# DeltaNet's head norms on one Trainium2 core: the sum of squares as two fp32r products over the high and low parts

## The reference

```python
def l2_normalize(x):
    xf = x.astype(jnp.float32)
    return xf * lax.rsqrt(jnp.sum(xf * xf, axis=-1, keepdims=True) + L2_EPS)

qkv = jax.nn.silu(causal_depthwise_conv(qkv, conv_w))
q, k, v = jnp.split(qkv, [GDN_QK_DIM, 2 * GDN_QK_DIM], axis=-1)
q = l2_normalize(q.reshape(B, T, 16, 128))
k = l2_normalize(k.reshape(B, T, 16, 128))
```

## Time and profile before

| | us |
|---|---|
| median of 3 runs | 2800.21 (2799.41 to 2800.48) |
| the profiled execution | 2803.94 |
| its span, first to last instruction | 2802.1 |
| PE busy | 2739.6 (98%) |
| DVE busy | 2219.6 (79%) |
| ACT busy | 1648.4 (59%) |
| mean granted TensorE clock | 0.995 |

### The profile page before, as it was taken

The page is one execution under the profiler, slowest core; times in us unless marked ns, Lnnn a source line. Parts: engine busy times, 40 slices in busy tenths (PEclk is TensorE's granted clock), DMA queues, the critical chain, the costliest instruction groups (busy, mean ns, idle before and its releaser), DMA issues.

```text
span 2802.1 us, 40252 instructions
## 1 busy us (share of the span) xinstructions
PE 2739.6 (98%) x13456; PEld 2282.1 (81%) x13456; DVE 2219.6 (79%) x2727; ACT 1648.4 (59%) x2184; POOL 31.0 (1%) x30
## 2 busy tenths in 40 slices
PE   8999999999988999999999999999999999999998
PEld 6878888888877888888888888888887888888887
DVE  5867877878767788888888876557677888888887
ACT  6766767667665555555555555554555555555554
POOL 0000000000000000000000000000000000000000
PEclk9999999999999999999999999999999999999999
DMA  6534444445433566656666656643345666656664
GB/s 239 181 124 153 159 144 163 156 149 167 158 105 113 166 210 199 198 185 203 198 198 203 198 172 224 222 135 114 106 158 188 207 199 200 199 184 200 198 201 166
DMA packets 135097, 493.23 MB, mean 176 GB/s; under 512 B 15009, under 2 KB 15329, under 8 KB 134625
## 3 DMA queue, kind: packets, MB, share of 16 engines
q1 hardware_dynamic: 133776, 487.82, 52.8%
q10 hardware_dynamic: 1232, 4.23, 0.4%
HBM read 489.86 MB, written 2.13 MB: 176 GB/s over the span
## 4 chain that ended last, share of the span: by engine, by line
PE 65%; issue 29%; DVE 3%; ACT 2%; DMA 1%; POOL 0%; POOLq 0%; DVEq 0%; SPq 0%; ACTq 0%
PE ACC L733 10%; PE ACC L735 10%; PE ACC L734 10%; PE SIDE L943 7%; PE SIDE L944 7%; PE SIDE L945 7%; PE ACC L943 3%; PE ACC L944 3%; PE ACC L945 3%; PE SIDE L741 2%; DVE W_LO L1627 1%; DMA RAW<-stream 1%; PE SIDE L1138 1%; ACT W_HI L1194 0%; ACT WORK L1587 0%
## 5 line engine op out<-in xcount | busy, mean ns | idle before, releaser
L1627 DVE TENSOR_TENSOR W_LO<-RAW,W_HI 128x1024 fp32r<-128x1024 f32 x424 | 511.6, 1222 | 268.9 <-ACT W_HI L1194 265.8
L1194 ACT ACTIVATE W_HI<-RAW 128x1024 fp32r<-128x1024 f32 x424 | 443.3, 1057 | 217.5 <-PE ACC L735 183.8
L1436 ACT ACTIVATE W_HI<-WORK 128x1024 fp32r<-128x1024 f32 x320 | 325.4, 1031 | 345.8 <-PE SIDE L945 232.7
L733 PE MATMUL ACC<-W_HI,X_HI 128*128 128x512 f32 x1216 | 491.2, 404 | 17.7 <-DVE W_LO L1627 17.6
L735 PE MATMUL ACC<-W_HI,X_LO 128*128 128x512 f32 x1216 | 477.6, 393 | 0.0
L734 PE MATMUL ACC<-W_LO,X_HI 128*128 128x512 f32 x1216 | 476.7, 392 | 0.0
L1878 DVE TENSOR_TENSOR W_LO<-WORK,W_HI 128x1024 fp32r<-128x1024 f32 x300 | 364.5, 1221 | 119.0 <-ACT W_HI L1436 116.3
L1436 ACT ACTIVATE W_HI<-RAW 128x1024 fp32r<-128x1024 f32 x328 | 314.8, 980 | 237.0 <-PE ACC L735 141.6
L733 PE MATMUL ACC<-W_HI,A_HI 128*128 128x512 f32 x928 | 370.3, 399 | 0.7 <-issue 0.7
L735 PE MATMUL ACC<-W_HI,A_LO 128*128 128x512 f32 x928 | 362.7, 391 | 0.0
L734 PE MATMUL ACC<-W_LO,A_HI 128*128 128x512 f32 x928 | 362.2, 390 | 0.0
(11 more groups left out here) (363 smaller groups left out, 3798.7 us busy)
## 6 DMA issues: line engine op xcount, KB each, us to landing
RAW<-stream SPq DMA_DIRECT2D x752, 512.0 KB, 4.6
WORK<-stream SPq DMA_DIRECT2D x160, 512.0 KB, 4.8
WORK<-gdn_rows ACTq DMA_DIRECT2D x8, 512.0 KB, 6.2
WORK<-xt SPq DMA_DIRECT2D x4, 512.0 KB, 9.3
H<-x SPq DMA_DIRECT2D x2, 1024.0 KB, 13.6
out<-WORK SPq DMA_DIRECT2D x4, 512.0 KB, 3.5
WORK<-tails SPq DMA_DIRECT2D x2, 512.0 KB, 10.8
WORK<-gfin SPq DMA_DIRECT2D x1, 1024.0 KB, 6.6
```

The lines of the kernel that those rows point to most:

```text
L733: nc.tensor.matmul(dst, hi[:, at:at + P], wh, start=first and h % 2 == 0 and q == 0, stop=False)
L1194: nc.scalar.activation(W_HI[:, h % WS, :], raw_piece(h), ACT.Copy).then_inc(hi_ready, 1)
L1436: nc.scalar.activation(dst, src, ACT.Copy).then_inc(hi_ready, 1)
L1627: nc.vector.tensor_tensor(W_LO[:, h % WS, :], raw_piece(h), W_HI[:, h % WS, :].bitcast(f32), SUB).then_inc(lo_ready, 1)
```

## The change

The tile of ones gets an fp32r copy, ONE_R, made once by ACT in iteration 0. The step squares on ACT now has two instructions: the square in f32 to cv, as before, and the square once more, rounded to fp32r, to B_HI. A new step sq_lo on DVE subtracts B_HI from cv and writes the rest to B_LO in fp32r. The step ss on PE waits for sq_lo and forms, for each half of 512 columns, two fp32r products, ones x B_HI and ones x B_LO, which add up in PSUM: four products in place of two f32 ones. In the tables, sq_lo takes the slot behind squares. ss goes from slot 18 to slot 19 in the looped iterations (ahead of decay) and in iteration 1; it stays at slot 17 in iteration 0 and at slot 18 in iteration 7.

```diff
 PREP_STEPS
     17 squares
-    18 ss
-    19 decay
+    18 sq_lo
+    19 ss decay
 FIRST_STEPS
     14 squares
+    15 sq_lo
     17 ss fill factors qkn
 PREP_1
     17 squares decay
-    18 ss
+    18 sq_lo
+    19 ss
 PREP_7
     16 silu_qk squares
+    17 sq_lo
     18 decay ss
...
+        ONE_R = sb("ONE_R", [P, P], f32r)
...
             elif name == "ss":
-                pe.wait_ge(sq_done, g + 1)
+                pe.wait_ge(sq_lo, g + 1)
                 for i in range(2):
-                    m = nc.tensor.matmul(dst[:, i * 512:(i + 1) * 512], ones, cv[:, i * 512:(i + 1) * 512], **ONE)
+                    half = slice(i * 512, (i + 1) * 512)
+                    nc.tensor.matmul(dst[:, half], ONE_R[:, :], B_HI[:, half], start=True, stop=False)
+                    m = nc.tensor.matmul(dst[:, half], ONE_R[:, :], B_LO[:, half], start=False, stop=True)
                 m.then_inc(side_full[p], 1)
...
                 act.wait_ge(silu_done, g * 2 + 1)
-                nc.scalar.activation(cv, cq, ACT.Square).then_inc(sq_done, 1)
+                nc.scalar.activation(cv, cq, ACT.Square)
+                nc.scalar.activation(B_HI[:, :], cq, ACT.Square).then_inc(sq_done, 1)
...
                     act.wait_ge(in_const, 16)
+                    nc.scalar.activation(ONE_R[:, :], ones, ACT.Copy)
                     tail_scalar(act, 0, tailraw)
...
+            elif name == "sq_lo":
+                dve.wait_ge(sq_done, g + 1)
+                nc.vector.tensor_tensor(B_LO[:, :], cv, B_HI[:, :].bitcast(f32), SUB).then_inc(sq_lo, 1)
```

More of the change, by code:

```diff
@@ L642, in build @@
          att_done, fin_mean, y_dve, y_act, out_done, dve_chain, pool_chain,
-         t_done, m1_out, mix, silu_f, hid_done, z_step, z_hi, z_lo, act_lo, cmp_out, t0_done, h_t0) = (sem(n) for n in (
+         t_done, m1_out, mix, silu_f, hid_done, z_step, z_hi, z_lo, act_lo, cmp_out, t0_done, h_t0, sq_lo) = (sem(n) for n in (
              "in_head in_const in_masks sm_zero x_first tail_in w2_in fin_in pad_zero hi_ready lo_ready w_used x_hi sumsq rstd tail_hi tail_lo "
@@ L648, in build @@
              "att_done fin_mean y_dve y_act out_done dve_chain pool_chain "
-             "t_done m1_out mix silu_f hid_done z_step z_hi z_lo act_lo cmp_out t0_done h_t0").split())
+             "t_done m1_out mix silu_f hid_done z_step z_hi z_lo act_lo cmp_out t0_done h_t0 sq_lo").split())
         x_in = [sem(f"x_in{i}") for i in range(NT)]
```

## The result

After the change the kernel takes 2808.53 us (median of 8 runs, 2806.60 to 2812.18) against 2800.35 us for the kernel before beside it (median of 8 runs, 2797.58 to 2803.29): a ratio of 1.003 with a 95% interval of 1.0019 to 1.0041. The forecast was 2801.4 us with a range up to 2807.0, so the time lies outside it, on the slower side.

What follows compares the result with a forecast made beforehand. TensorE, busy 98% of the span, was taken as the bound. Iteration 0 +0.4, iteration 1 -0.6, looped iterations +0.6 and iteration 7 +0.8 summed to +1.2 us: median 2801.4 us, range 2795.5 to 2807.

Steps and rivals of the forecast that it cites:

- The cheaper product: Ones product at ss: four fp32r products cost 1.00 us instead of 1.77, saving 0.77 us an iteration.
- The order in the loop: Iterations 2 to 6: ss waits 0.89 us for v0's copy-out, net +0.12 each, +0.6 us over five.
- (b): Rival: s comes late out of ACT in the loop, ks waits about 1.2 us five times; 2807.3 us, chance 0.10.
- Iteration 0: Crowded slots 14 and 15: ss waits 1.1 us for the subtraction; +0.4 us.
- Iteration 1: v0 waits for ru's sum, ss for v0's copy-out; low clock moves, giving back time; -0.6 us.
- the low stretch: Iteration 1, 161.4 to 164.8 us at clock 0.52: expected to fall on v0 and ss, giving back about 1 us.
- Iteration 7: Saving hidden behind ACT, second Square adds 0.97, low clock ending where it did returns a part; +0.8 us.
- the length of ss: Iteration 7: ss's last product ends at 813.45, just as Ln's table load does; v0 starts near 814.7.
- (a): Rival: the product's saving of 6.2 us stays whole, the new wait and Square hidden; 2794.0 us, chance 0.08.
- (d): Rival: the ones products keep the old pace, 0.77 us more in seven iterations; 2806.8 us, chance 0.04.
- (c): Rival: shifted waits remove or add two low-clock stretches of 1.7 us each; 2798.0 or 2804.8 us, chance 0.12.

Runs made afterwards that it cites:

- e8: Changed kernel with ss at slot 18 in looped iterations and iteration 1, old f32 ones product, second Square and subtraction kept: 2806.59 us, 1.0023.
- e3: Changed kernel with ss back at slot 18 (sq_lo at 17) in the looped iterations and iteration 1: 2802.37 us, 1.0011.
- e2: The changed kernel, unchanged, run again for a second profile: 2810.06 us, 1.0035.
- e5: Changed kernel with iteration 7 alone as before (one Square, no sq_lo, f32 ones product): 2804.0 us, 1.0016.
- e10: e5 with the second Square of iteration 7 left in, its result unused: 2805.04 us, 1.0017.
- e11: Changed kernel with the subtraction sq_lo of iteration 7 one slot earlier (slot 16): 2804.81 us, 1.0018.
- e13: Kernel before with only the order changed, ss behind v0 (slot 19), in the looped iterations alone: 2805.97 us, 1.0023.
- e9: Kernel before with the new product in looped iterations only (sq_lo slot 17, ss 18), decay behind ss in iterations 1 and 7: 2794.64 us, 0.9981.
- e7: Kernel before with decay moved behind ss (slot 19) in iterations 1 and 7 only: 2798.63 us, 0.9994.
- e15: Kernel before with only the order changed, ss behind v0 in looped iterations and iteration 1; one profiled execution: 2806.28 us.
- e16: The same program as e15, profiled once more: 2812.15 us.

## Why the forecast was wrong

**The cheaper product: right.** 0.76 us an iteration measured, 0.77 forecast (e8 against e3).

**The order in the loop: mechanism right, term too small by half.** The wait stands where the forecast put it and ks doesn't wait, so rival (b) is false, and s is out 0.3 us before ks. +1.3 us instead of +0.6 over five: 1.82 and 1.03 where I took 1.79 and 1.00 gives 0.06 of the missing 0.13 an iteration. Another 0.06 is a term that the sum left out: with ss gone from slot 18, the first weight product behind ru has a pitch of 0.29 (370.17 to 370.46) and not 0.23. In the kernel before, the slow first pitch stood behind ss, and the forecast took it away with ss, inside the 2.00 us. The table loads behave as the trace said: from the load at 377.19 to Exp at 378.48 it is 1.29 us, as in the earlier trace rows, and s is out before ks. With the drain that the Trainium skill gives ("ScalarE: Activation LUTs", What ACT_TABLE_LOAD costs), ks would have waited some 2.6 us, an estimate; it waits for nothing, so the measurement decides against it here.

**Iteration 0: right in place.** ss waits 0.90 us for the subtraction (1.1 forecast; -0.77 + 1.1 is +0.3, not the +0.4 written there):

```profile
71.56 0.48 PE L845 MATMUL SIDE<-B_HI,ONE_R 128*128 128x512 f32 x1 [0.90 <-DVE B_LO L1760]
```

and the stretch is 0.4 to 0.8 us longer in the two profiles. Over all profiles, ru of iteration 1 starts at 155.76 to 156.55 us where iteration 0 is the changed one (after, e2, e3, e5, e10, e11) and at 155.01 to 155.77 where it is the old one.

**Iteration 1: the failed step is "I expect the low stretch to fall on v0 and ss".** The waits came as said, the first below for ru's sum, the second for v0's copy-out, but the low stretch did not move, it grew. It took in ss (records of 0.63 us, at 162.05 for one) and the products behind it:

```profile
159.04 1.16 PE L790 MATMUL SIDE<-WORK 128*128 128x128 f32 x8 [1.40 <-DVE WORK L1830]
161.46 0.80 PE L845 MATMUL SIDE<-B_HI,ONE_R 128*128 128x512 f32 x1 [1.26 <-ACT VN L1205]
...
159.20:162.60 3.40, 2.14 (x11) 1.73 (x11) 2.06 (x2) 3.38 (x4) 0.00 (x0) 0.62 0.41 145
162.60:166.00 3.40, 3.40 (x10) 2.66 (x9) 0.00 (x0) 2.51 (x3) 0.00 (x0) 0.50 0.48 154
```

Two stretches at 0.62 and 0.50, against one at 0.52 in the earlier trace rows. Three more profiles have this iteration 1 (e5 100.65 us, e10 101.26, e11 101.07). With them it is +0.2 to +0.9 us instead of -0.6, a miss of 0.8 to 1.5. Part of that is scatter of the clock: before's own iteration 1 came out at 99.11 in e13.

**Iteration 7: the failed step is the length of ss.** The forecast had the subtraction end 3.6 us after ru; it ended 3.60 after (815.36 and 811.76). It had Ln's table loaded 4.87 us after ru; that too came out (816.63). But it let the four products run at the full pace, 1.25 us, and they took 2.05 at 1.2 GHz, so v0 came 6.99 us after ru, not 6.12. e11, whose ss runs at full clock, has 6.06. (Its stretch of 90.35 us is 0.8 more than before, as forecast, but that is luck: e10, with the same place of v0, has 91.53.) The rest of the term is the clock behind: +1.9 us in one profile, +5.4 in the other, where the forecast had the low clock end "where it did". In the second, 0.50 and 0.58 stand behind each other (818.00 to 824.80) with PE busy almost throughout.

**The sum.** The order in the loop explains 0.7 of the 7 us by which the median missed, iteration 1 from 0.8 to 1.5, and iteration 7 from 1.1 to 4.6, depending on the execution. The last is of the size that e11 and e5 give back in the median. That the low clock has a part agrees with the timed runs: their mean granted clock is 0.997 before (0.9968 over the 104 runs beside the experiments), 0.994 and 0.993 after and again, and 0.997 in e9. 0.003 of 2800 us is 8.4 us of full pace, an upper bound for what it can cost, as PE also waits at low clock. The mean clock alone doesn't give the time: e3 has 0.994 as well and is some 5 us faster, which is what its order saves in the loop.

**Rivals.** (a) was right about the size of the product's saving (e3's loop) and false about the outcome. (b), the late s, is false. (d) is false: the products do keep the fp32r pace. (c) was the one that came, on its slower side; I gave it 0.12, spread to both sides, and priced it by stretches added or removed at random. Its price of +3.4 us for two more stretches gives 2804.8 us, below every run after (2806.6 the fastest), so it is too small by itself. And the new waits spoke for one direction: the change puts three new waits on PE beside stretches of low clock (iteration 1 twice, iteration 7; the earlier trace rows), and that the low stretch would move and not grow had no row behind it.

**Open.** What decides whether an execution falls into the longer group, and whether it is the clock alone. The 3 us or so of e8 that its profile doesn't show. The 0.6 and 1.6 us in the rest of the span of after, which can't be told from the spread of that stretch. And whether moving decay alone (e7) gains anything in the median.

## What to carry to other kernels

Here the cheaper product paid in full where TensorE was the bound and no other step used its PSUM tile in that slot: the same four products gave 3.7 us in the loop at slot 18 and cost 1.3 at slot 19, behind another step's copy-out. The instructions that split the operand for it were free only where their engines idled. So try such a change first in the loop, where it is hidden, and leave the crowded first and last iterations as they are: that took 2794.6 us against 2808.5 (e9, which also moves decay, so not all of it is due to this). Where a new wait falls on a thinly busy stretch, price it together with the clock behind it, at both levels, and profile such a kernel more than once.

## What the runs showed of the hardware

- The same steps, behind the same wait of 2.11 us, ran on at a granted clock of 0.52 for 3.4 us in one execution (before) and at 1.00 in another (e13); the iteration took 100.44 and 99.11 us.
- One program gave two groups of times, 2805.0 to 2806.7 and 2809.9 to 2811.9 us. Between e15 (2806.28) and e16 (2812.15), 5.2 of the 5.9 us lie in two stretches of 90 to 100 us in which the granted clock differs by 0.03 and 0.05 while DVE and ACT work the same time.
- A wait of 0.93 us of v0 in a thinly busy place cost some 4 us of the median (3.2 to 5.6; after against e11).
- At 1.2 GHz the four fp32r products of 128x512 took 2.05 us to the end of the last record, against 1.20 at full clock in the loop.
